# Modulation operations laid over two iterations, idle products at stage borders, last norm by row tiles

## What is computed

```python
mod = (silu(c) @ ada_w[layer] + ada_b[layer]).reshape(B, 3, 3, 1024)   # shift, scale, gate of 3 sublayers
h = rms_norm(x, g) * (1 + scale) + shift
x = x + 0.5 * gate * swiglu(h, w_in, w_down)       # sublayers 0 and 2 of each layer, 2816 wide
x = x + gate * mixer(h)                            # sublayer 1: attention in layer 0, HGRN in layer 1
...
h = rmsnorm(x, norm_g)                             # second block
x = x + concat(gla, sparse attention, pooling)(h @ w_in) @ w_out
return rmsnorm(x, final_norm_g)                    # x * rsqrt(mean(x * x) + 1e-6) * gain, by token
```

## Time and profile before

| | us |
|---|---|
| median of 3 runs (2556.3 to 2557.11) | 2556.78 |
| the profiled execution, its own time | 2561.48 |
| its span, first to last instruction | 2559.9 |
| TensorE busy | 2451.6 (96%) |
| VectorE busy | 1249.2 (49%) |
| ScalarE busy | 878.2 (34%) |
| GpSimd busy | 178.3 (7%) |
| DMA queue of the weights (SyncE), share of the 16 DMA engines | 27.9% |
| DMA queue of the modulation tiles (GpSimd) | 8.6% |

### The profile page before, as it was taken

One profiled execution on the slowest core, in us unless ns is written; L12 is line 12 of the kernel. 1 busy time (PEld: TensorE's weight loads), 2 busy tenths in 40 slices (PEclk: granted clock), 3 DMA queues, 4 the chain that ended last, 5 costly groups with the idle time before them and its releaser, 6 DMA issues.

```text
span 2559.9 us, 30543 instructions
## 1 busy us (share of the span) xinstructions
PE 2451.6 (96%) x11102; PEld 1937.5 (76%) x11102; DVE 1249.2 (49%) x1904; ACT 878.2 (34%) x1320; POOL 178.3 (7%) x307
## 2 busy tenths in 40 slices
PE   7999999899889999999999989999999999999997
PEld 3788888666567888878888868888788888767666
DVE  4775333545567664343333344554533333468453
ACT  3222222555532222223322233334322222343442
POOL 2111000000001110000000003331000000100000
PEclk9999999999999999999999999999999999999989
DMA  6986332211128883323333322122233333321211
GB/s 241 305 257 219 106 105 83 91 56 52 42 77 278 255 268 115 100 72 90 98 98 108 97 69 63 50 58 75 77 104 98 93 115 87 70 72 48 70 42 50
DMA packets 419782, 285.25 MB, mean 111 GB/s; under 512 B 22612, under 2 KB 397710, under 8 KB 419700
## 3 DMA queue, kind: packets, MB, share of 16 engines
q1 hardware_dynamic: 397312, 207.64, 27.9%
q0 software_dynamic: 20896, 73.80, 8.6%
q10 hardware_dynamic: 1492, 2.74, 0.3%
HBM read 277.26 MB, written 6.68 MB: 111 GB/s over the span
## 4 chain that ended last, share of the span: by engine, by line
PE 86%; DVE 6%; ACT 3%; issue 2%; DMA 1%; DVEq 0%; POOL 0%; ACTq 0%
PE bank L573 12%; PE bank L575 12%; PE bank L574 12%; PE bank L731 6%; PE bank L733 6%; PE bank L732 6%; PE bank L1289 4%; PE bank L1291 4%; PE bank L1290 4%; PE bank L1316 2%; PE bank L948 1%; PE bank L608 1%; PE bank L610 1%; PE bank L609 1%; PE bank L972 1%
## 5 line engine op out<-in xcount | busy, mean ns | idle before, releaser
L533 DVE TENSOR_TENSOR w_lo<-raw,w_hi 128x1024 fp32r<-128x1024 f32 (+1 forms) x333 | 435.2, 1307 | 433.8 <-ACT w_hi L515 426.8
L573 PE MATMUL bank<-h_hi,w_hi 128*128 128x512 f32 x1344 | 527.8, 393 | 9.4 <-DVE w_lo L533 7.3
L515 ACT ACTIVATE w_hi<-raw 128x1024 fp32r<-128x1024 f32 (+1 forms) x333 | 371.5, 1116 | 455.6 <-PE bank L575 224.2
L574 PE MATMUL bank<-h_lo,w_hi 128*128 128x512 f32 x1344 | 523.9, 390 | 0.0
L575 PE MATMUL bank<-h_hi,w_lo 128*128 128x512 f32 x1344 | 523.9, 390 | 0.0
L573 PEld LDWEIGHTS bank<-h_hi,w_hi 128*128 128x128 f32 x1344 | 252.7, 188 | 68.0 <-DVE w_lo L533 14.0
L575 PEld LDWEIGHTS bank<-h_hi,w_lo 128*128 128x128 f32 x1344 | 252.7, 188 | 53.6
L574 PEld LDWEIGHTS bank<-h_lo,w_hi 128*128 128x128 f32 x1344 | 252.9, 188 | 51.5
L731 PE MATMUL bank<-g_hi,w_hi 128*128 128x512 f32 x704 | 277.4, 394 | 0.0
L733 PE MATMUL bank<-g_hi,w_lo 128*128 128x512 f32 x704 | 276.0, 392 | 0.0
L732 PE MATMUL bank<-g_lo,w_hi 128*128 128x512 f32 x704 | 273.2, 388 | 0.0
(11 more groups left out here) (374 smaller groups left out, 3100.1 us busy)
## 6 DMA issues: line engine op xcount, KB each, us to landing
raw<-in_ffn_w_in SPq DMA_DIRECT2D x176, 512.0 KB, 3.8
ada<-in_ada_w POOLq DMA_DIRECT2D x128, 512.0 KB, 5.3
raw<-in_ffn_w_down SPq DMA_DIRECT2D x64, 704.0 KB, 4.5
raw<-in_hgrn_w_in SPq DMA_DIRECT2D x32, 512.0 KB, 4.1
raw<-in_attn_w_qkv SPq DMA_DIRECT2D x24, 512.0 KB, 3.8
raw<-in_w_in SPq DMA_DIRECT2D x22, 512.0 KB, 3.8
ada_first<-in_ada_w SPq DMA_DIRECT2D x16, 512.0 KB, 15.8
raw<-in_attn_w_o SPq DMA_DIRECT2D x8, 512.0 KB, 3.7
```

The lines of the kernel that those rows point to most:

```text
L515: line(nc.scalar.activation(w_hi[:, n % 2, 0:k * P], raw[:, n % 4, 0:k * P], ACT.Copy), hi_ready)
L533: line(nc.vector.tensor_tensor(w_lo[:, n % 2, 0:k * P], raw[:, n % 4, 0:k * P], w_hi[:, n % 2, 0:k * P].bitcast(F32), ALU.subtract), lo_ready)
L573: nc.tensor.matmul(out_ap, wh, xh, start=(k == 0), stop=False)
L574: nc.tensor.matmul(out_ap, wh, xl, start=False, stop=False)
```

## The change

It has three parts.

1. Modulation. A part now lies over two iterations. Iteration m does operation 0 behind the gating product of half 0, operations 1, 2, 3 between the splits of half 1 and operation 4 behind its gating product; iteration m + 1 does operations 5, 6, 7 between the splits of its half 0, and TensorE does the eight small products after the two blocks of that half. The first iteration only begins a part, and one more iteration, written out, ends the last.
2. Idle products. `norm_pe` gets four fp32 products of 128 columns of ones with ones, into a bank that nobody reads, between the two sums (norms 1 to 6), and fourteen behind the second.
3. Last norm. `norm_pe`, `norm_act` and `norm_dve` aren't called for m = 7. VectorE multiplies each tile j of the result by its gain as soon as its residual is there, TensorE turns it back one block later (`final_turn`), ScalarE copies it to x_rows (`final_copy_act`). At the end the sums are taken with one column per row tile, so that they lie by token; Ln and Exp are of 128x4; ScalarE scales row tiles 0 and 2, VectorE 1 and 3, each in three pieces, and SyncE stores in eight DMAs of 256 KB.

```diff
@@ ffn_pe
-            def up(n, i, m, with_ada):
+            def up(n, i, m, ada_end):
                 for s in range(2):
...
                     for b in range(2):
                         product(pe, n + 2 * s + b, B[2 * s + b][:, :], H_TILES, i)
-                if with_ada:
-                    ada_pe(pe, q0 + m, i)
-            up(n0, None, 0, parts > 0)
+                    if ada_end and s == 0:
+                        ada_pe(pe, q0 + m - 1, i)
+            up(n0, None, 0, False)
             if parts:
                 with pe.Fori(0, parts - 1) as i:
                     up(n0 + 4, i, 1, True)
-            k = max(parts, 1)
+                up(n0 + 4 * parts, None, parts, True)
+            k = parts + 1
@@ ffn_dve, up
                     if m or s:
                         split_lo(dve, line, n + 2 * s + 1, i)
-                    if with_ada:
-                        for kk in ((0, 1, 2), (5, 6, 7))[s]:
+                    if ada_end and s == 0:
+                        for kk in (5, 6, 7):
+                            ada_dve(dve, line, q0 + m - 1, kk, i)
+                    if ada_begin and s == 1:
+                        for kk in (1, 2, 3):
                             ada_dve(dve, line, q0 + m, kk, i)
                     split_lo(dve, line, n + 2 * s + 2, i)
...
                     line(nc.vector.tensor_tensor(tmp[:, s, :], sq[:, :], B[2 * s + 1][:, :], ALU.mult), gt_ready)
-                    if with_ada:
-                        for kk in ((3, 4), ())[s]:
-                            ada_dve(dve, line, q0 + m, kk, i)
+                    if ada_begin:
+                        ada_dve(dve, line, q0 + m, 4 * s, i)
@@ norm_pe
+        def idle_turns(count):
+            for _ in range(count):
+                nc.tensor.matmul(B[7][:, 0:P], ones[:, :], ones[:, :], start=True, stop=True)
...
             nc.tensor.matmul(B[5][:, :], ones[:, :], sumsq[:, :], start=True, stop=False)
+            if m:
+                idle_turns(4)
             pe.wait_ge(sq_ready, KD * (m + 1))
             nc.tensor.matmul(B[5][:, :], ones[:, :], sq[:, :], start=False, stop=True).then_inc(rms_ps, 1)
+            if 0 < m < 7:
+                idle_turns(14)
@@ the last norm
+        FIN = ((0, 4), (4, 7), (7, 8))
...
+        def final_gain_dve(dve, line, j):
+            line.settle()
+            if j >= 2:
+                dve.wait_ge(fin_ps, j - 1)
+            line(nc.vector.tensor_scalar(tmp[:, j % 2, :], xT[:, j, :], cols[:, 0, 56 + j:57 + j], None, ALU.mult), fin_t)
+        def final_turn(pe, j):
+            pe.wait_ge(fin_t, j + 1)
+            if j >= 2:
+                pe.wait_ge(fin_cp, j - 1)
+            for t in range(TT):
+                s = slice(t * P, (t + 1) * P)
+                bank = B[4] if j == KD - 1 and t % 2 else B[2 + j % 2]
+                last = nc.tensor.transpose(bank[:, s], tmp[:, j % 2, s], ident[:, :])
+            last.then_inc(fin_ps, 1)
+        def final_copy_act(act, line, j):
+            act.wait_ge(fin_ps, j + 1)
+            line(nc.scalar.activation(x_rows[:, :, j * P:(j + 1) * P],
+                                      B[2 + j % 2][:, :].rearrange("p (t n) -> p t n", n=P), ACT.Copy), fin_cp)
+        def final_pe(pe):
+            final_turn(pe, KD - 2)
+            pe.wait_ge(sum_ready, (KD - 1) * 8)
+            for t in range(TT):
+                last = nc.tensor.matmul(B[5][:, t:t + 1], sumsq[:, t * P:(t + 1) * P], ones[:, 0:1], start=True,
+                                        stop=True)
+            last.then_inc(rms_ps, 1)
+            pe.wait_ge(sq_ready, KD * 8)
+            for t in range(TT):
+                last = nc.tensor.matmul(B[6][:, t:t + 1], sq[:, t * P:(t + 1) * P], ones[:, 0:1],
+                                        start=True, stop=True)
+            last.then_inc(rms_ps, 1)
+            final_turn(pe, KD - 1)
...
+        def final_act(act, line):
+            act.wait_ge(fin_sum, 1)
+            line(nc.scalar.activation(small[:, 60:64], small[:, 60:64], ACT.Ln, bias=eps_c, scale=1.0 / D))
+            line.settle()
+            line(nc.scalar.activation(small[:, 60:64], small[:, 60:64], ACT.Exp, scale=-0.5), rstd_ready)
+            line.settle()
+            act.wait_ge(fin_ps, KD)
+            for t in (0, 2):
+                for a, b in FIN:
+                    line(nc.scalar.activation(x_rows[:, t, a * P:b * P], final_source(t, a, b), ACT.Copy,
+                                              scale=token_rstd(t)), fin_even)
...
@@ second_pe
+            final_turn(pe, 0)
             for j in range(2, KD):
                 out_part(pe, j, tuple(range(9)))
+                if j < KD - 1:
+                    final_turn(pe, j - 1)
@@ residual_dve
+            if n >= FIRST["OUT"]:
+                final_gain_dve(dve, line, j)
@@ back_act
                 residual_act(act, line, FIRST[name] + j, KD * RES_OF[name] + j + 1, j)
+                if name == "OUT" and j:
+                    final_copy_act(act, line, j - 1)
@@ sync
             for t in range(TT):
-                sp.wait_ge(fin_sb, 2 * (t + 1))
-                sp.dma_start(out[0, t * P:(t + 1) * P, :], tmp_out(t)).then_inc(out_done[t % 2], 16)
+                scaled = fin_odd if t % 2 else fin_even
+                for half, parts in ((0, 1), (1, 3)):
+                    sp.wait_ge(scaled, 3 * (t // 2) + parts)
+                    cs = slice(half * T, (half + 1) * T)
+                    sp.dma_start(out[0, t * P:(t + 1) * P, cs], x_rows[:, t, cs]).then_inc(out_done[half], 16)
```

More of the change, by code:

```diff
@@ L359, in program @@
         fin_ps = sem("fin_ps")
-        fin_sb = sem("fin_sb")
+        fin_cp = sem("fin_cp")
+        fin_sum = sem("fin_sum")
+        fin_even = sem("fin_even")
+        fin_odd = sem("fin_odd")
         out_done = [sem(f"out_done{i}") for i in range(2)]
@@ L403, in landings, with token_rstd @@
             return 16 * total
-        def tmp_out(t):
-            return tmp[:, 2 * (t % 2):2 * (t % 2) + 2, :]
+        FIN = ((0, 4), (4, 7), (7, 8))
+        def token_rstd(t):
+            return small[:, 60 + t:61 + t]
+        def final_gain_dve(dve, line, j):
[12 more added lines that the diff above has]
+            last.then_inc(fin_ps, 1)
@@ new lines, in final_dve @@
+        def final_dve(dve, line):
+            dve.wait_ge(rms_ps, 8)
+            line(nc.vector.tensor_copy(small[:, 60:64], B[5][:, 0:TT]))
+            dve.wait_ge(rms_ps, 9)
+            line.settle()
+            line(nc.vector.tensor_tensor(small[:, 60:64], small[:, 60:64], B[6][:, 0:TT], ALU.add), fin_sum)
+            dve.wait_ge(rstd_ready, 8)
+            dve.wait_ge(fin_cp, KD - 1)
+            dve.wait_ge(fin_ps, KD)
+            for t in (1, 3):
+                for a, b in FIN:
+                    line(nc.vector.tensor_scalar(x_rows[:, t, a * P:b * P], final_source(t, a, b), token_rstd(t), None,
+                                                 ALU.mult), fin_odd)
@@ L860, in ffn_dve, with up @@
             n0 = FIRST[name]
-            def up(n, i, m, with_ada):
+            def up(n, i, m, ada_end, ada_begin):
                 for s in range(2):
@@ L883, in ffn_dve @@
             per = ((lo_ready, 4), (gt_ready, 2), (g_ready, 2))
-            up(n0, None, 0, parts > 0)
-            line.loop(1, parts, lambda i: up(n0 + 4, i, 1, True), per + ((ada_used, 8),))
-            k = max(parts, 1)
-            line.loop(k, KF // 2 - 1, lambda i: up(n0 + 4 * k, i, k, False), per)
-            up(n0 + 4 * (KF // 2 - 1), None, KF // 2 - 1, False)
+            up(n0, None, 0, False, parts > 0)
+            line.loop(1, parts, lambda i: up(n0 + 4, i, 1, True, True), per + ((ada_used, 8),))
+            if parts:
+                up(n0 + 4 * parts, None, parts, True, False)
+            k = parts + 1
+            line.loop(k, KF // 2 - 1, lambda i: up(n0 + 4 * k, i, k, False, False), per)
+            up(n0 + 4 * (KF // 2 - 1), None, KF // 2 - 1, False, False)
             if parts:
@@ L2366, in _ @@
             for t in range(TT):
-                sp.wait_ge(fin_sb, 2 * (t + 1))
-                sp.dma_start(out[0, t * P:(t + 1) * P, :], tmp_out(t)).then_inc(out_done[t % 2], 16)
-            for i in range(2):
-                sp.wait_ge(out_done[i], 16 * TT // 2)
+                scaled = fin_odd if t % 2 else fin_even
[3 more added lines that the diff above has]
+                    sp.dma_start(out[0, t * P:(t + 1) * P, cs], x_rows[:, t, cs]).then_inc(out_done[half], 16)
+            for half in range(2):
+                sp.wait_ge(out_done[half], 16 * TT)
         @block.gpsimd
@@ L2479, in _ @@
             back_act(act, line, "OUT")
-            norm_act(act, line, 7, None)
-            for t in range(TT):
-                act.wait_ge(fin_ps, t + 1)
-                if t >= 2:
-                    act.wait_ge(out_done[t % 2], 16 * (t // 2))
-                for hf in range(2):
-                    line(s.activation(tmp[:, 2 * (t % 2) + hf, :], B[2 * (t % 2) + hf][:, :], ACT.Copy), fin_sb)
```

(16 more changed lines are left out.)

8 lines of the change are left out of this document (4 added, 4 removed).

## The result

The changed kernel took 2523.92 us (median of 4 runs, 2522.96 to 2524.88), the kernel before 2556.95 us beside it (4 runs, 2556.3 to 2558.77): ratio 0.987, 95% interval 0.9853 to 0.9887. The forecast of 2519.4 lay 4.5 us under it, and its range, 2514 to 2533, held it. The profiled execution of after took 2524.68 us with a span of 2523.1, 36.8 us less than the span of before.

A forecast was written before the change was run, and what follows sets the result against it. TensorE, with 86% of the chain of waits, was taken as the bound. Gains of 16.6 + 13.3 + 7.5 = 37.4 us off the 2556.8 us median gave 2519.4 us, range 2514 to 2533.

The forecast's parts named there:

- part 1, F0: F0's feed-forward up stage: moving modulation operations regains all TensorE waiting, 9.1 us of its 21.9 us surplus over F2.
- part 1, F1: F1's feed-forward up stage: moving modulation operations regains all TensorE waiting, 7.5 us of its 24.0 us surplus over F2.
- part 2, six pairs: Opening product pairs behind norms 1 to 6: idle products keep full clock, 11.0 us a pair, 13.3 us gained.
- part 3, the end: From last product to kernel end: last norm by row tiles shortens 21.2 us to 11.0, gain 10.2 us.
- part 3, five turns: Four transposes per turn among the output products: five turns at 0.54 us each cost 2.7 us.
- the pattern of the earlier trace: Looped parts of F0 and F1: two modulation operations after the gating product delay w_lo; 14 times 0.7 us, 9.8 us.
- The slack of 0.8 us at operation 4: Second half of an iteration: with one operation after the gating product, w_lo ends at 4.6 us, needed at 5.44.
- The other place: Next block's split behind operations 5 to 7: w_lo ends at 9.7 us, needed at 10.9, slack 1.2 us.
- The first iteration of F0: Late modulation tiles hold up block 2's split, TensorE idles 2.12 us; split and gating product now precede operation 0.
- Rival (a): Norm borders: idle products do not hold the clock; 2532.7 us, or 2549.5 if it falls at once; chance 0.12.
- fourteen fit by 0.3 us: Between second sum and pair at each border: fourteen idle products take 3.1 us of the 3.41 us left.
- Rival (d): Up stages: modulation tiles land too late, operation 0 tightest, making the kernel slower, up to 2603 us; chance 0.02.

The follow-up runs named there:

- the 49 runs: The kernel before, unchanged, in all runs that stood beside the experiments: 2555.76 to 2568.40 us, median 2559.08 us.

## Why the prediction was right, and what it missed

| step | forecast | trace before minus after |
|---|---|---|
| part 1, F0 | 9.1 | 250.38 - 241.41 = 9.0 |
| part 1, F1 | 7.5 | 252.51 - 245.10 = 7.4 |
| part 2, six pairs | 13.3 | 86.11 - 72.76 = 13.35 |
| part 3, the end | 10.2 | 21.17 - 11.54 = 9.6 |
| part 3, five turns | -2.7 | 5 x 0.44 = -2.2 |
| sum | 37.4 | 37.2 |

No mechanism that the sum rests on failed in the traces. The span of the profiled execution fell by 36.8 us; between this and 37.2 stand stages that no part touches: start and first pair 1.4 us longer, attention 1.3 longer, the small-state and output products 2.3 shorter apart from the turns. That these nearly cancel is luck: in the second trace of the changed kernel the same stages moved by 1.7, 1.3, 1.2 and 0.7 us against its first.

**The point taken from.** The step that was off is the last: "I take them from the median: 2556.8 - 37.4". The rows were of an execution of 2561.48 us. Less 37.4 that is 2524.1; the measured median is 2523.9, closer than the 36.8 of the spans would give. Taken from the 49 runs' median of 2559.1 it would have been 2521.7. Three runs within 0.8 us of each other looked more certain than they were: later runs lay up to 12 us above. So 2.3 of the 4.5 us of error come from that sample. The other 2.2 are within the noise of the four runs (their ratio is known to 0.17%, 4 us); that they are the clock in stages that no step speaks of is argued, not shown.

**Part 1.** The forecast of 16.6 us was right for the trace it was read from (16.4); against the five traces with the old places it would be 14.8 to 18.4. The prediction put the pattern of the earlier trace rows at 14 places, and the trace has it at just these 14, with 0.39 to 0.41 us. The slack of 0.8 us at operation 4 was 0.85. The other place, before the block behind the small products, I put at 1.2 us of slack; it has 3.0 (the split of 797.09 ends at 798.31, TensorE wants it behind the small products at 801.3), because the small products come ahead of that block. I had counted those 1.7 us for the other half of the iteration. It changed nothing. The first iteration of F0, which I had only argued (the split and the gating product ahead of operation 0), has no recorded wait of TensorE left, and F0 gained all its 9 us. Operation 0 does wait for the small products, 0.19 us, and costs nothing.

**Part 2.** Rival (a), that such idle products would not hold the clock, had 0.12 and was the largest. The traces refute it: in the ten traces with such products (or transposes, or only seven) none of the 60 pairs behind a border has a slow product, and in the four traces without them each of the 24 has 5 to 12. The sentence that fourteen fit by 0.3 us was right: with 28 the delay is 2.86 us, fourteen took 3.29, so the room was 0.4. What I didn't see is that seven may be enough.

**Part 3.** The rows of the end, ScalarE and the output DMAs of the changed kernel, counterpart of the earlier trace rows:

```profile
2511.17 0.39 PE L1801 MATMUL bank<-h_hi,w_lo 128*128 128x512 f32 x1
...
2514.35 0.30 ACT L461 ACTIVATE small<-small 128x4 f32<-128x4 f32 x1 [0.85 <-DVE small L477]
2514.68 0.21 ACT L463 ACTIVATE small<-small 128x4 f32<-128x4 f32 x1
2514.92 1.23 ACT L468 ACTIVATE x_rows<-x_rows,small 128x512 f32<-128x512 f32 x2
...
2515.67 4.58 SPq L2466 DMA_DIRECT2D out<-x_rows  x8
...
out<-x_rows SPq DMA_DIRECT2D x8, 256.0 KB, 2.6
```

The last product ends at 2511.56, the first piece starts 3.4 us later (forecast 3.3), the first DMA goes 4.1 later (3.9), the end is at 11.5 (11.0). Ln and Exp of 128x4 took 0.30 and 0.21 us, for which I had set 0.25 each, between 0.15 and 0.63. The remaining 0.3 us are the data: 373 to 389 GB/s in windows of 1 us while the DMAs ran, not 400. A turn cost 0.44 us (blocks 6.61 us apart instead of 6.17), the bare four transposes, without the restart of 0.1 that I had added.

**Rival (d)**, modulation tiles landing too late, would have shown a wait of VectorE for ada in the up stages. The trace has none, and the median landing is 5.1 us, where it was 5.3.

## What to carry to other kernels

In front of an engine that is the bound, cost a moved operation by the slack of the one consumer behind it (start of the block, its length, end of the split), not by its share of an iteration: one operation of 1.3 us more behind the gating product cost 13 us. Where TensorE waits and then runs at half clock, cheap products into an unread bank during the wait give back the slow ones behind it; count how many fit, since each one too many is paid in full, and look for such stretches in the whole kernel: nine further places gave 12 us here, where the six borders gave 13. One trace does not tell whether a short wait is safe, since the same wait went both ways between executions. Subtract a sum of rows from the execution that the rows are of, or from many runs, not from three.

## What the runs showed of the hardware

- A wait of TensorE for 1.58 us behind 7 idle products left the clock at 1.00 at six borders of one trace. One of 1.63 us behind four transposes was followed by 7 products at half clock in five of eight traces and by none in three, and went both ways in two traces of one program. Left open.
- fp32 transposes hold the granted clock as fp32 products do (28 in 3.22 us, the pair behind them at 0.39 us a product and a clock of 1.00).
- Executions of one program differ by 12 us (2555.76 to 2568.40), and the time goes with the mean granted clock, 2555.8 to 2558.1 us at 0.983 and 2565.2 to 2568.4 at 0.977. With idle products at fifteen places the mean clock was 0.994 to 0.997.
- The fp32 products at the start ran for 8 us at a clock of 0.57 after a wait of 1.95 us, though TensorE was busy for 7.45 of the 8 us. With 8 idle products in that wait the clock was 1.00, beside the same 410 GB/s of loads.
